# Where a norm's root is applied: from the rows of the input to the results of the products

## The reference

```python
def rmsnorm(x, g):
    y = xf * lax.rsqrt(jnp.mean(xf * xf, axis=-1, keepdims=True) + NORM_EPS)
    return y * g

h = rmsnorm(x, g_mix);  u = h @ w_in            # conformer convolution, gated delta net
x = x + mixed @ w_out
m = rmsnorm(mem, g_mem); mk, mv = m @ w_mk, m @ w_mv      # keys, values, also outputs
x = x + cross_attn(rmsnorm(x, g_xattn), mk, mv, w_xq, w_xo)
x = x + moe(rmsnorm(x, g_moe), ...)             # router: top 4 of 32 experts, clamped SwiGLU
y = rmsnorm(x, g_final)
```

## Time and profile before

| | us |
|---|---|
| median of 3 runs (1396.79 to 1402.38) | 1400.07 |
| the profiled execution | 1404.49 |
| its span, first to last instruction | 1402.8 |
| PE busy | 1332.7 (95%) |
| DVE busy | 466.0 (33%) |
| ACT busy | 232.1 (17%) |
| first product behind the input norm starts | 25.9 |
| expert loop's first gather starts | 449.9 |
| last scattered result arrives, final norm begins | 1381 to 1384 |

### The profile page before, as it was taken

One profiled execution on the slowest core, in us unless ns is written; L12 is line 12 of the kernel. 1 busy time (PEld: TensorE's weight loads), 2 busy tenths in 40 slices (PEclk: granted clock), 3 DMA queues, 4 the chain that ended last, 5 costly groups with the idle time before them and its releaser, 6 DMA issues.

```text
span 1402.8 us, 17717 instructions
## 1 busy us (share of the span) xinstructions
PE 1332.7 (95%) x6683; PEld 644.9 (46%) x6683; DVE 466.0 (33%) x1328; ACT 232.1 (17%) x444; POOL 33.0 (2%) x69
## 2 busy tenths in 40 slices
PE   6989898999887999999999999999999999999997
...
GB/s 309 126 60 61 1 222 61 194 238 266 302 404 108 289 429 426 429 428 427 429 428 427 428 430 427 427 431 427 427 431 427 427 431 427 427 430 429 427 430 38
DMA packets 56508, 469.47 MB, mean 335 GB/s; under 512 B 6828, under 2 KB 7061, under 8 KB 31885
## 3 DMA queue, kind: packets, MB, share of 16 engines
...
...
## 4 chain that ended last, share of the span: by engine, by line
PE 86%; DMA 5%; DVE 5%; ACT 2%; issue 1%; ACTq 1%; DVEq 0%; POOL 0%; SPq 0%; POOLq 0%
PE bank L928 51%; PE bank L516 10%; PE bank L974 5%; DMA ring<-in_w_gu 5%; PE bank L743 4%; PE bank L941 3%; PE bank L960 2%; PE bank L526 2%; PE bank L954 1%; DVE ring L1604 1%; ACTq L1042 1%; PE bank L646 1%; PE bank L654 1%; PE bank L714 1%; PE bank L723 1%
## 5 line engine op out<-in xcount | busy, mean ns | idle before, releaser
L928 PE MATMUL bank<-ring,region_p 128*64 128x512 f32 x2304 | 504.8, 595 | 1.9 <-DMA ring<-in_w_gu 1.2
L928 PEld LDWEIGHTS bank<-ring,region_p 128*64 128x64 f32 x2304 | 163.4, 137 | 327.4 <-issue 323.3
L1755 DVE TENSOR_SCALAR region_p<-bank 128x512 f32<-128x512 f32 x32 | 22.1, 692 | 615.7 <-PE bank L960 615.7
L928 PE MATMUL bank<-region_m,region_p 128*64 128x512 f32 x768 | 169.5, 593 | 0.5 <-DMA region_m<-in_w_gu 0.5
L516 PE MATMUL bank<-hT,ring 128*128 128x264 f32 x512 | 119.1, 392 | 1.1 <-ACT region_m L1132 1.1
L1732 DVE TENSOR_TENSOR xT<-xT,bank 128x264 f32<-128x264 f32 x264 | 95.5, 424 | 60.5 <-PE bank L974 60.5
L516 PEld LDWEIGHTS bank<-hT,ring 128*128 128x128 f32 x512 | 98.0, 194 | 18.7 <-ACT region_m L1132 1.5
L928 PEld LDWEIGHTS bank<-region_m,region_p 128*64 128x64 f32 x768 | 54.4, 137 | 108.6 <-issue 107.3
L928 PE MATMUL bank<-region_p 128*64 128x512 f32 (+1 forms) x396 | 99.7, 622 | 3.8 <-DVE region_p L1717 3.8
L1273 ACT COPY region_p<-bank 128x264 f32<-128x264 f32 x33 | 12.5, 378 | 475.3 <-PE bank L954 475.3
L974 PE MATMUL bank<-region_p 64*128 64x264 f32 x528 | 81.0, 415 | 0.5 <-ACT region_p L1273 0.5
...
## 6 DMA issues: line engine op xcount, KB each, us to landing
...
```

Source lines behind the costliest of these rows:

```text
L928: ins = pe.matmul(bank[n][u * SLOTS:(u + 1) * SLOTS, :], lhs, rhs, start=start, stop=stop)
L1755: dve.tensor_scalar(xg, bank[0][:, :], 7.0, None, ALU.min).then_inc(sem("glu_clipped"), 1)
```

## The change

For the memory, attention and MoE norms, products take x times gain, and the root of each token is multiplied in where tokens lie on partitions: at the drains of mk, mv, q_s and h_tok, as the scale of the softmax's Exp, and in the addition of the router's bias. The square sums of the attention and MoE norms are made of one summed tile of squares and a few products two columns wide (`token_sums`), with tokens on partitions, and stand behind q_s and behind logits in PE's list. Memory's square sums are made by ACT along the free dimension of the token rows.

For the input norm, ACT and DVE take the square sums of the token rows, scale the rows, and PE transposes the scaled rows (`xn_t`) and then the plain ones (`x_t`). The gain is applied as hT is drained. The input is loaded in three DMAs. For the final norm PE transposes the chunks of xT as they are finished; ACT squares the banks with a sum along the free dimension, DVE multiplies the banks by root and gain; the gain comes by an added broadcast DMA on POOL, and is no longer among ACT's parameter loads (11 in place of 12 on that semaphore).

ACT loads one table that holds Ln and Exp, by name, in place of letting each function load its own.

```diff
-    jobs = [("x_t", c) for c in range(8)]
-    jobs += [("param", 0), ("param", 1), ("mix_norm",), ("short_hist",), ("ab",), ("qkv", 0), ("ab_t",)]
-    jobs += [("qkv", f) for f in range(1, 4)] + [("conv_hist", j) for j in range(2)]
+    jobs = [("param", 0)] + [("xn_t", c) for c in range(8)] + [("x_t", c) for c in range(8)]
+    jobs += [("param", 1), ("qkv", 0), ("short_hist",), ("ab",), ("qkv", 1), ("ab_t",)]
+    jobs += [("qkv", f) for f in range(2, 4)] + [("conv_hist", j) for j in range(2)]
...
-    jobs += [("s_outer", g) for g in range(sample_groups)] + [("mem_norm",)]
+    jobs += [("s_outer", g) for g in range(sample_groups)]
...
-    jobs += [("w_out", d) for d in range(8)] + [("x_norm",)]
-    jobs += [("q_s",)] + [("xq", d) for d in range(8)] + [("s_score_t",)]
+    jobs += [("w_out", d) for d in range(8)]
+    jobs += [("q_s",), ("x_norm",)] + [("xq", d) for d in range(8)] + [("s_score_t",)]
...
-    jobs += [("xo", d) for d in range(8)] + [("moe_norm",)]
-    jobs += [("logits",), ("h_tok", 0), ("h_tok", 1), ("logits_t",)] + [("h_tok", i) for i in range(2, 6)]
+    jobs += [("xo", d) for d in range(8)]
+    jobs += [("logits",), ("moe_norm",), ("h_tok", 0), ("h_tok", 1), ("logits_t",)] + [("h_tok", i) for i in range(2, 6)]
...
-            sp.dma_start(x_tok[:, 0:2, :], x_prompt[0].rearrange("(t p) d -> p t d", p=P)).then_inc(sem("x_in"), 16)
-            sp.dma_start(x_tok[0:TS, 2, :], x_sample[:, 0, :]).then_inc(sem("x_in"), 16)
+            sp.dma_start(x_tok[:, 0, :], x_prompt[0, 0:P, :]).then_inc(sem("x0_in"), 16)
+            sp.dma_start(x_tok[0:TS, 2, :], x_sample[:, 0, :]).then_inc(sem("xs_in"), 16)
+            sp.dma_start(x_tok[:, 1, :], x_prompt[0, P:2 * P, :]).then_inc(sem("x1_in"), 16)
...
+            pool.dma_start(g_bc, g_final.rearrange("(o n) -> o n", o=1).to_broadcast([P, D])).then_inc(sem("g_bc_in"), 16)
...
+            def token_sums(key, sq, s, copies):
                 open_bank(pe, key)
-                for i, k in enumerate(order[:n]):
-                    if ready is not None:
-                        pe.wait_ge(sem(ready), i + 1)
+                pe.wait_ge(sem(s), 1)
+                for t in range(NT):
+                    pe.matmul(ps(key)[:, 2 * t:2 * t + 2], sq[:, t * P:(t + 1) * P], ones[:, 0:2], start=True, stop=True)
+                for j in range(copies):
+                    m = pe.matmul(ps(key)[32 * j:32 * j + 32, 2 * NT:2 * NT + 2], sq[:, TP:TP + 32], ones[:, 0:2],
+                                  start=True, stop=True)
+                filled(m, key)
...
-            open_bank(pe, ("fin_norm",))
             pe.wait_ge(sem("hg_ready"), n_items + 2)
-            column_sums(("fin_norm",), x_sq, KT, T, "x4_sq", ADD_ORDER)
-            for i in range(6):
-                key = ("y_t", i)
-                t, hf = divmod(i, 2)
-                _, r0, m = ROWS[t]
-                open_bank(pe, key)
+            for n, d in enumerate(ADD_ORDER):
+                pe.wait_ge(sem("scat_added"), 8 * n_items + (n + 2))
+                hf, u = divmod(d, 4)
+                for t, r0, m in ROWS[0:NT]:
+                    key = ("y_t", 2 * t + hf)
+                    ins = pe.transpose(ps(key)[:, u * P:(u + 1) * P], xT[:, d, r0:r0 + m], ident[:, :])
+                    if u == 3:
+                        filled(ins, key)
+            t, r0, m = ROWS[NT]
+            for hf in range(2):
+                key = ("y_t", 2 * t + hf)
                 for u in range(4):
-                    pe.wait_ge(sem("h_fin"), 4 * hf + u + 1)
-                    ins = pe.transpose(ps(key)[0:m, u * P:(u + 1) * P], hT[:, 4 * hf + u, r0:r0 + m], ident[:, :])
+                    ins = pe.transpose(ps(key)[0:m, u * P:(u + 1) * P], xT[:, 4 * hf + u, r0:r0 + m], ident[:, :])
...
+            def ln_exp_table():
+                act.preload_act_table_set("natural_log_exp_and_others")
...
+            def gain_and_square(kind, d, gain, sq, h_sem, sq_sem):
+                wait_drained(act, kind, d)
+                act.mul(hT[:, d, :], xT[:, d, :], pcol(gain, d)).then_inc(sem(h_sem), 1)
+                act.activation(sq[:, d * T:(d + 1) * T], xT[:, d, :], ACT.Square).then_inc(sem(sq_sem), 1)
+            def token_roots(key, n, dst, s, bias):
+                wait_filled(act, *key)
+                link(act.activation(dst[0:n, :], ps(key)[0:n, 0:6:2], ACT.Ln, bias=eps_t[0:n, 0:1], scale=1.0 / D))
+                drained(act.activation(dst[0:n, :], dst[0:n, :], ACT.Exp, scale=-0.5, bias=bias), key)
+                wait_drained(act, *key)
+            ln_exp_table()
+            act.wait_ge(sem("x0_in"), 16)
+            act.activation(xn_tok[:, 0, :], x_tok[:, 0, :], ACT.Square, accum_out=x_ss[:, 0:1]).then_inc(
+                sem("x_ss"), 1)
             act.wait_ge(sem("const"), 1)
-            act.preload_act_table(ACT.Ln)
-            squares(xT, lambda k: wait_drained(act, "x_t", k), "x_sq", T)
-            inv_root(("mix_norm",), T, 1.0 / D)
+            act.wait_ge(sem("x_ss"), 3)
+            link(act.activation(x_rs, x_ss, ACT.Ln, bias=eps_t[:, 0:1], scale=1.0 / D))
+            act.activation(x_rs, x_rs, ACT.Exp, scale=-0.5).then_inc(sem("x_rs"), 1)
+            act.wait_ge(sem("x_rs"), 1)
+            act.mul(xn_tok[:, 1, :], x_tok[:, 1, :], x_rs[:, 1:2]).then_inc(sem("xn1"), 1)
...
+            for c in range(1, 8, 2):
+                wait_filled(act, "xn_t", c)
+                drained(act.mul(hT[:, c, :], ps(("xn_t", c))[:, 0:T], pcol("mix", c)), ("xn_t", c))
+            for c in range(1, 8, 2):
+                wait_filled(act, "x_t", c)
+                drained(act.copy(xT[:, c, :], ps(("x_t", c))[:, 0:T]), ("x_t", c))
...
-                drained(act.copy(memT[:, c, :], ps(("mem_t", c))[:, 0:NMEM]), ("mem_t", c))
-            squares(memT, lambda k: wait_drained(act, "mem_t", k), "mem_sq", NMEM, mkT)
-            inv_root(("mem_norm",), NMEM, 1.0 / D)
-            act.preload_act_table(ACT.Ln)
...
+                drained(act.mul(memT[:, c, :], ps(("mem_t", c))[:, 0:NMEM], pcol("mem", c)), ("mem_t", c))
+            act.wait_ge(sem("mem_in"), 16)
+            for t in range(2):
+                link(act.activation(mkT[:, 4 * t:4 * t + 4, :].rearrange("p c n -> p (c n)"), mem_tok[:, t, :],
+                                    ACT.Square, accum_out=m_ss[:, t:t + 1]))
+            link(act.activation(m_rs, m_ss, ACT.Ln, bias=eps_t[:, 0:1], scale=1.0 / D))
+            link(act.activation(m_rs, m_rs, ACT.Exp, scale=-0.5))
             for j in range(4):
                 hf, t = divmod(j, 2)
                 wait_filled(act, "mk", j)
-                drained(act.copy(mk_tok[:, t, hf * 512:(hf + 1) * 512], ps(("mk", j))[:, :]), ("mk", j))
+                drained(act.mul(mk_tok[:, t, hf * 512:(hf + 1) * 512], ps(("mk", j))[:, :], m_rs[:, t:t + 1]),
+                        ("mk", j))
...
+            for d in range(8):
+                gain_and_square("w_out", d, "xattn", x2_sq, "h_xattn", "x2_sq")
+            token_roots(("x_norm",), P, x2_rs, "x2_rs", eps_t[:, 3:4])
             wait_filled(act, "q_s")
             for h in range(XH):
-                ins = act.copy(q_s[:, h * XD:(h + 1) * XD], ps(("q_s",))[32 * h:32 * h + TS, 0:XD])
+                ins = act.mul(q_s[:, h * XD:(h + 1) * XD], ps(("q_s",))[32 * h:32 * h + TS, 0:XD],
+                              x2_rs[32 * h:32 * h + TS, 2:3])
...
+                gain_and_square("xo", d, "moe", x3_sq, "h_moe", "x3_sq")
...
+            link(act.activation(x3_rs[:, 0:2], ps(("moe_norm",))[:, 0:4:2], ACT.Ln, bias=eps_t[:, 0:1], scale=1.0 / D))
+            link(act.activation(x3_rs[0:TS, 2:3], ps(("moe_norm",))[0:TS, 4:5], ACT.Ln, bias=eps_t[0:TS, 0:1],
+                                scale=1.0 / D))
+            act.activation(x3_rs[:, 0:2], x3_rs[:, 0:2], ACT.Exp, scale=-0.5)
+            drained(act.activation(x3_rs[0:TS, 2:3], x3_rs[0:TS, 2:3], ACT.Exp, scale=-0.5), ("moe_norm",))
...
+            def final_root(t):
                 m = ROWS[t][2]
+                act.wait_ge(sem("f_sum"), t + 1)
+                link(act.activation(f_rs[0:m, t:t + 1], f_sum[0:m, t:t + 1], ACT.Ln, bias=eps_t[0:m, 0:1],
+                                    scale=1.0 / D))
+                act.activation(f_rs[0:m, t:t + 1], f_rs[0:m, t:t + 1], ACT.Exp, scale=-0.5).then_inc(sem("f_rs"), 1)
+            def final_squares(t, hf):
+                m = ROWS[t][2]
+                i = 2 * t + hf
                 wait_filled(act, "y_t", i)
-                drained(act.copy(y_out[0:m, t, hf * 512:(hf + 1) * 512], ps(("y_t", i))[0:m, :]), ("y_t", i))
+                if i < 4:
+                    squared = hT.rearrange("p a b -> p (a b)")[0:m, i * 512:(i + 1) * 512]
+                else:
+                    squared = (rn, sig)[i - 4].rearrange("p a b -> p (a b)")[0:m, 0:512]
+                act.activation(squared, ps(("y_t", i))[0:m, :],
+                               ACT.Square, accum_out=f_ss[0:m, i:i + 1]).then_inc(sem("f_ss"), 1)
```

(50 more changed lines are left out.)

173 lines of the change are left out of this document (92 added, 81 removed).

## The result

The changed kernel took 1384.72 us in the median of four runs (1381.68 to 1386.9) against 1399.76 for the one before, ratio 0.989 (0.986 to 0.992); in a second set of runs, beside the kernel before on its chip (1402.96 there), 1382.85 us in five runs (1381.48 to 1385.19), ratio 0.986 (0.984 to 0.988). It is 15 to 20 us faster, and the forecast was 1384.5. Its profiled execution took 1386.9 us with a span of 1385.2, 17.6 less than before's 1402.8.

The account below looks back on a forecast made before the run. PE and weight transfers nearly tie in the expert loop, so earlier work shifts the end. Terms 9.4 - 2.6 - 6.4 - 5.2 - 5.7 - 5.1 = -15.6 took profiled 1404.5 to 1388.9, or 1384.5 as median; range 1376 to 1392.

Parts of the forecast that it names:

- Start: Input norm to qkv 1: waiting for ACT's queue and a second set of transposes cost 9.4 us, bounds +1.2 to +11.0.
- first rival: Start: PE's clock rises during the long transposes or stays up after decay; up to 8.2 us less, about 1378; chance 0.13.
- Decay: Decay and unit vectors: two table loads of 1.28 us go, -2.6 us, bounds 0 to -6.
- Memory norm: Between last s_outer and first mk product: sums, Ln, load, Exp and scaling go, -6.4 us, bounds -5 to -6.4.
- Attention norm: Behind w_out: q_s runs at once, narrow sums follow, roots enter its drains; -5.2 us, bounds -4 to -6.
- MoE norm: Between xo and the router's bias add: logits run at once, narrow sums follow; -5.7 us, bounds -4.5 to -6.
- End: Final norm: x transposed as it is added up, ACT squares and DVE scales banks; -5.1 us, bounds -3.5 to -6.
- the prediction's sign: What the changed profile would show, including nine table loads instead of 25.
- Loop: Expert loop: same length as now, entered 10.5 us earlier than 449.9.
- second rival: Expert loop bound by weights swallows gains ahead of it; only the final norm's -5.1 stays, 1395 us; chance 0.08.
- the slower one: Expert loop's DMA pace worsens: gain gone at 1.7% more per piece, 1407 us at 2.5%; chance 0.04.
- the half gain: Norms' gains come to half through short waits or cold PE at narrow products: 1389 to 1393 us; chance 0.15.

Follow-up runs that it names:

- first experiment: Kernel before, with Ln and Exp from one activation table and the norms left as they were: 1387.86 us, ratio 0.990; repeated 1387.49 us, ratio 0.990.
- late-loads kernel: Changed kernel with x transposed first, ACT's last six loads issued behind the input norm, DVE making all PSUM copies there: 1371.38 us, ratio 0.978.

## Why the prediction was right, and where it was not

The sum was right to 2 us in the first profile (17.6 against 15.6), 6 us off in the second (21.5), and the time within 2 us of both medians. In the second set that is luck: the kernel before took 2.9 us more on that chip, and the gain was 20.1. The steps hold in kind (each norm's wait went as forecast, and the start paid), less so in size. By its own steps, measured in the first profile and the second:

- Start, forecast +9.4: +9.5 and +5.9. Two errors cancelled in the first. **ab** was put at 3.4 us from before's row and took 1.04: there it had been paced by DVE's scaled rows one by one (3.37 again in the kernel with the old start), while its 16 records, 32 columns wide and placed in four groups of columns, take less than a third of 16 full ones (3.57) when their input is ready. Against that the issue of br_bc was taken as fixed (ScalarE free at 15.0) and ran to 17.07. ScalarE's free moment differed by 3.5 us between two executions of this kernel, which belonged into the range. With ScalarE free at 15.0 the start would have cost 7.4 and not 9.4. The transposes (0.82 per group) and the slow first tile (+2.0, measured 2.2 and 2.1; 1.0 to 2.2 in the other forms of this start) were right: 13.4 us of transposes did not raise the pace of the tile behind them, which is what the Trainium skill (TensorE: Matmul & The Clock Gate, Part 4, PE-mode transpose) says of them; by its closing table the tile would have taken 3.6, not 5.7. The slowness is read from durations alone: the granted clock in the profile reads 1.00 from 20 to 42 us, while a transpose took 0.28 us there and 0.13 behind xo (8 in 1.02). The lower bound of this term was worked out with 0.43 us for a group of three such transposes; by the row it cites they take 0.38, which makes it +0.4 and not +1.2. Only the range and the first rival use it.
- Decay, −2.6: −2.84 both times, the two loads and 0.3 of gaps between ScalarE's instructions. The kk products behind the shorter wait took 1.14 instead of 2.06; they fall into the next stretch.
- Memory norm, −6.4: −6.37. Attention norm, −5.2: −4.8 and −4.5, q_s 3.57 instead of 4.4 and the sums 0.76 instead of 1.3, the four scaled drains 1.9 in all instead of 1.7 (0.46 to 0.48 each against 0.36 to 0.38 unscaled), and the write 3.33 instead of 2.11 beside the bulk load, which the upper bound (−4) had allowed for. MoE norm, −5.7: −6.9, since the logits (L560 in the changed kernel's timeline of PE) took 1.84 and not 3.4, the same mistake as with ab. End, −5.1: −4.5. Table loads fell from 26 to 10 by the traces; the prediction's sign had 25 and nine.
- Loop, unchanged: −0.2 and −0.4. It was entered 12.9 us earlier (10.5 forecast) and left 13.1 earlier, so the second rival (the loop swallows the gain) is refuted, and so is the slower one, by the same row. The warm start and the half gain, rivals one and four, are refuted by the start and by the memory and MoE stretches.
- Not in the sum: the recurrence, 1.4 us shorter both times, and up to 5 shorter in other kernels, without an edit there. All of the 1.4 lies at its start: kk 0.92 less, and the four records behind it (L663 in the changed kernel) 0.63 instead of 1.09. The prediction had that only as a bound of its decay term (up to 3.4). Further on two batches of 64 records took 10.0 to 11.7 and 8.2 to 9.6 us in different kernels, with a granted clock of 0.62 and 0.85 around them in the changed kernel; what sets it stays open.

What the prediction did not see is the balance. The loads, taken away alone, are worth 13.6 and 14 us by the ratios, where the first experiment's theory counted 7 × 1.28 = 9.0 and the prediction had no sum for them. The norms' new form then wins 5.1 (memory), 5.6 (MoE), 1.8 to 2.4 (attention) and 3 (end), and loses 9 to 13 at the start (9.0 of it its own, the rest ScalarE's free moment) and 3 in xo, where only the one-table kernel kept the clock. On top of the tables the rest of the change is worth 1 to 6 us, by the ratios 0.9903 and 0.9899 against 0.9892 and 0.986; the intervals of the first pair overlap, so that alone would not tell it from nothing. And of the start's loss none was necessary: it named ScalarE's queue and the second set of transposes as what the start waits for, but costed both as given. In the late-loads kernel z0 ends at 72.28, 5 ahead of before, with the new norm's arithmetic unchanged.

Left open: why the issue of one small load takes 1.8 us in one execution and 5.2 in the next, and what decides the clock behind a given idle time.
